# Router logits from the unnormalised residual, the shared expert split around the ranking and among the routed experts, and a smaller table of relative biases

## The chip, the cores and the metric

The kernel runs on one core of one Trainium2 chip. The metric is the device time of one launch in microseconds (us). Five engines work side by side: TensorE (PE, with its weight loads PEld), VectorE (DVE), ScalarE (ACT), GpSimd (POOL) and SyncE (SP, which here only issues transfers). They wait for one another through semaphores.

## The reference, cut to what matters

Two blocks run one after the other on 512 tokens of width 1024, in float32. The first has a gated mixer, attention with a relative bias, and two convolutional feed-forwards. The second has two more mixers and then a mixture of experts:

```
h = rms_norm(x, norm2_g) * (1 + sc2) + sh2
scores = sigmoid(h @ router_w)                      # 64 experts
sel = scores + router_bias                          # choice: 4 of 8 groups, then 6 experts
idx = top_6(sel in the 4 best groups)
wts = scores[idx] / sum(scores[idx]) * 2.5
routed = sum over idx of wts * swiglu(h, exp_w[idx])
shared = swiglu(h, sh_w_gate, sh_w_up, sh_w_down)   # for every token, inner width 256
x = x + g2 * (routed + shared);  out = rms_norm(x, final_g)
```

The attention of the first block adds `b_rel_bias[head, distance]` to its scores, for 16 heads and distances up to 256.

## The kernel before, in words

Activations lie transposed in on-chip memory: features on the 128 partitions, in 8 blocks (`KB`), and the 512 tokens along the free dimension. One float32 product of a 128x128 weight tile with 512 columns is shown as two matmul records. A transpose of 128x128 is one record.

Order is set by hand. Each engine has one program, and `s("name")` with a count says what it waits for. Four places matter here.

The table of relative biases. GpSimd writes the 16 x 384 row `relR` 128 times per head to `rel_dram` (3 MB), then reads it back skewed as `biasT` (128 partitions, 2 MB), lines 625 to 630. In that time the "gv" stage runs: TensorE takes four units of `a_w_in` of 1 MB through a ring of two buffers (L940). SyncE issues the load of a unit when the buffer's last reader is done (L438).

The first output projection, "go" (L845). The weights come in four units of two output blocks each. The first four output blocks are computed together, k by k over `gT`, as VectorE produces it; the load of the third unit waits for the first unit's two outputs.

The norm of the second block (L1083 to L1095), then the projections (L1104) that follow a short chain on ACT and DVE.

The router stage. VectorE adds the last projection to x (L2424). ACT squares it (L1604), GpSimd sums six blocks (L641), TensorE sums over partitions (L827). ACT takes the root, VectorE the reciprocal of 128x512 (L2165) and the eight scalings (L2167), ACT the shifts (L1615). TensorE then computes the logits (L1417), turns the tokens for the gather (L1428), runs the shared gate and up products (L1436), the counts (L1443, L1445), the shared down products in pieces (L1458), the places of the tokens (L1491, L1498, L1501), and turns the result back (L1514). VectorE ranks (L2446 to L2468) meanwhile. Then come 44 expert units (L1531 gate and up, L1544 down). Units 0 to 3 have one expert with 128 slots, and after them units with two experts of 64 slots and units with one expert alternate. SyncE keeps four buffers of 3 MB filled: the two parts for the expert four places later are loaded when `exp_gu` and `exp_down` say that they are free (L505).

Of the kernel before, what the change touches and what calls it, by code (L numbers as in the profile page):

```python
# [91 lines left out]
def program(nc, a, out):  # L92

    with ExitStack() as ctx:
# [35 lines left out]
        rel_dram = scratch("rel_dram", 16, P, RELW + 1)  # L130
# [86 lines left out]
        sh_gu, sh_dn = flat_ring[:, 1024:5120], sqf[:, 2048:4096]  # L217
        hrow = [flat_ring[:, 1024 + D * n:1024 + D * n + D] for n in range(2)]
# [35 lines left out]
        xact = sqf[:, 0:1024].rearrange("p (b t) -> p b t", b=2)  # L254
# [156 lines left out]
        OV = 15  # L411

# [11 lines left out]
        def _(sp):  # L424
# [87 lines left out]
            for q in range(2):  # L512
                expert_in(q, bass.ds(q, 1), sems_of(q), slice(0, 3))
            expert_in(2, bass.ds(2, 1), sems_of(2), GU)
# [4 lines left out]
            expert_in(2, bass.ds(2, 1), sems_of(2), DN)  # L519
            sp.wait_ge(s("norm_ss_ready"), nth("n2"))  # L520
            sp.dma_start(sh_dn.rearrange("p (k n) -> p k n", k=2),
                         a["sh_w_down_2"][0].rearrange("(k p) n -> p k n", p=P)).then_inc(s("sh_loaded"), 16)
            sp.wait_ge(s("front_stored"), 48)
            expert_in(3, bass.ds(3, 1), sems_of(3), GU)
            sp.wait_ge(s("sh_prod"), 4 + KB)
            expert_in(3, bass.ds(3, 1), sems_of(3), DN)

            sp.wait_ge(s("rt_step"), 7)
# [37 lines left out]
        def _(pool):  # L566
# [37 lines left out]
            for n in range(6):  # L604
# [26 lines left out]
            pool.wait_ge(s("rel_stored"), 32)  # L631
# [3 lines left out]
            def square_sums(n):  # L635

                for b in range(1, KB - 1):
# [100 lines left out]
            square_sums("n2")  # L738
# [39 lines left out]
            pool.wait_ge(s("sh_prod"), 4)  # L778
# [12 lines left out]
            gather(0)  # L791
            gather(1)
            pool.wait_ge(s("sh_prod"), 4 + KB)
# [25 lines left out]
        def _(pe):  # L819
# [272 lines left out]
            pe.wait_ge(s("side_loaded"), 64)  # L1092
            for k in range(KB):
# [317 lines left out]
            mean_squares("n2")  # L1411
            pe.wait_ge(s("side_loaded"), 64)
            for t in range(TT):
                for k in range(KB):
                    if t == 0:
                        pe.wait_ge(s("norm_h_ready"), h_count("n2", k))
                    mm = pe.matmul(ps[0][:, t * 64:t * 64 + 64], hT[:, k, t * P:(t + 1) * P], rwt[:, k, :],  # L1417
                                   start=(k == 0), stop=(k == KB - 1))
            mm.then_inc(s("rt_prod"), 1)

            pe.wait_ge(s("mod_ready"), ADA_UNITS)
            pe.transpose(ps[1][0:8, 0:P], mod[:, 40:48], ident[:]).then_inc(s("rt_prod"), 1)

            for t in range(TT):
                for half in range(2):
                    wait(pe, s("tokens_taken"), 2 * (t - 1) + half + 1)
                    for b in range(4):
                        tr = pe.transpose(ps[2 + half][:, b * P:(b + 1) * P], hT[:, 4 * half + b, t * P:(t + 1) * P], ident[:])  # L1428
                    tr.then_inc(s("tokens_turned"), 1)

            pe.wait_ge(s("sh_loaded"), 48)
            w8 = sh_gu.rearrange("p (m k n) -> p m k n", m=2, k=KB)
            for m in range(2):
# [1215 lines left out]
```

## Time and profile before

| | us |
|---|---|
| three runs | 2834.86, 2831.92, 2834.57 (median 2834.57) |
| profiled execution, its own time | 2836.34 |
| its span | 2834.6 |
| TensorE busy | 2641.1 (93%) |
| VectorE busy | 839.5 (30%) |
| mean granted TensorE clock | 0.971 |

The span is the traced part of the profiled execution, 1.7 us shorter than its own time. Lines as L906 are lines of the kernel file. "Idle before" is the time for which the engine stood still ahead of a group, with what released it. A granted clock of 1.00 is 2.4 GHz, one of 0.50 is 1.2 GHz.

### The profile page before, as it was taken

The page shows a single profiled execution, that of the slowest core. Times are in us where ns is not written, and L with a number is a line of the kernel's source. Part 1 is how long each engine was busy: PE and PEld are TensorE (multiplying, and loading weights), DVE is VectorE, ACT ScalarE, POOL GpSimd, SP SyncE. Part 2 cuts the span into 40 slices and gives each one's busy share as a digit, 9 for nine tenths or more (in the row PEclk, how much of TensorE's full clock was granted, in tenths as well). Part 3 has the DMA queues.
Part 4 walks back from the last instruction along what each step waited for, and adds up shares of the span by engine and source line. Part 5 has one row for each costly group of instructions (what it writes and reads, how often), then busy time and mean ns, then how long its engine had stood idle before and what let it go on. Part 6 is the DMA issues. An engine that isn't in the chain of part 4 may idle for free. (4 is left out here: it accounts for less than half of the span.)

```text
span 2834.6 us, 27215 instructions
## 1 busy us (share of the span) xinstructions
PE 2641.1 (93%) x9849; PEld 1370.8 (48%) x9849; DVE 839.5 (30%) x1957; ACT 578.4 (20%) x1076; POOL 441.6 (16%) x397
## 2 busy tenths in 40 slices
PE   6999999999999999999999989999989999999992
PEld 5544444444566444444444447666745444344440
DVE  1023222102333232220022335556533322222215
ACT  2111111111333211110025533122111211111111
POOL 3004555500000100000121001101110111111110
PEclk9999999999999999999999999999988999999996
DMA  7315555432121122233232110000032799999985
GB/s 144 118 60 146 147 148 148 138 82 62 49 60 60 60 74 74 81 85 82 63 82 75 40 49 25 25 30 16 23 154 91 263 419 417 404 400 400 389 349 215
DMA packets 290831, 407.24 MB, mean 144 GB/s; under 512 B 14258, under 2 KB 253560, under 8 KB 264608
## 3 DMA queue, kind: packets, MB, share of 16 engines
q1 hardware_dynamic: 273504, 366.24, 37.3%
q0 software_dynamic: 16112, 37.19, 4.5%
q10 hardware_dynamic: 1104, 2.31, 0.2%
q8 instruction: 71, 1.16, 0.2%
q14 instruction: 40, 0.33, 0.0%
HBM read 396.20 MB, written 30.46 MB: 151 GB/s over the span
## 5 line engine op out<-in xcount | busy, mean ns | idle before, releaser
L906 PE MATMUL bank<-hT,bring 128*128 128x512 f32 x1344 | 582.1, 593 | 0.0
L906 PEld LDWEIGHTS bank<-hT,bring 128*128 128x128 f32 x1344 | 253.8, 190 | 311.9 <-issue 311.9
L845 PE MATMUL bank<-bring 128*128 128x512 f32 x704 | 303.3, 593 | 0.0
L1531 PE MATMUL bank<-bring 128*64 128x512 f32 (+1 forms) x512 | 227.0, 596 | 2.7 <-issue 1.7
L845 PEld LDWEIGHTS bank<-bring 128*128 128x128 f32 x704 | 133.5, 190 | 166.5 <-issue 166.5
L2023 DVE SCALAR_TENSOR_TENSOR ffw<-bank,col,ffw 128x511 f32<-128x511 f32 x88 | 66.0, 750 | 413.5 <-ACT ffw L1632 413.3
L1632 ACT ACTIVATE ffw<-bank,col 128x512 f32<-128x512 f32 x88 | 68.5, 778 | 492.7 <-PE bank L906 470.0
L2008 DVE TENSOR_TENSOR xT<-bank,xT 128x512 f32<-128x512 f32 x32 | 22.1, 691 | 377.3 <-PE bank L845 377.2
L1544 PE MATMUL bank<-bring,xT 128*64 128x512 f32 (+1 forms) x256 | 120.3, 614 | 9.1 <-DMA ysq<-exp_w_down 4.5
L1531 PEld LDWEIGHTS bank<-bring 128*64 128x64 f32 (+1 forms) x512 | 77.8, 157 | 97.4 <-issue 96.2
L1104 PE MATMUL bank<-hT,bring 128*128 128x512 f32 x256 | 118.5, 610 | 3.6 <-DVE ysq L2188 3.6
L641 POOL TENSOR_TENSOR ysq<-ysq 128x512 f32<-128x512 f32 x24 | 30.5, 1269 | 583.4 <-ACT ysq L1604 582.3
L1531 PE MATMUL bank<-ysq,bring 128*64 128x512 f32 (+1 forms) x256 | 113.4, 596 | 2.8 <-issue 2.8
L2563 DVE TENSOR_TENSOR xT<-bank,ysq 128x512 f32<-128x512 f32 x88 | 60.9, 692 | 180.1 <-PE bank L1544 180.1
L1531 PE MATMUL bank<-two,bring 128*64 128x512 f32 (+1 forms) x256 | 113.4, 596 | 0.5 <-issue 0.4
L1953 ACT ACTIVATE xT<-bank 128x256 f32<-128x256 f32 x44 | 16.9, 385 | 468.2 <-PE bank L1531 468.2
L735 POOL TENSOR_TENSOR ffw<-two,maskT 128x512 f32<-128x512 f32 x40 | 52.2, 1314 | 385.6 <-DVE two L2362 318.6
L656 POOL TENSOR_TENSOR two<-two,csil 128x2048 f32<-128x2048 f32 x24 | 86.5, 3604 | 154.9 <-DMA two<-ada_w 137.7
L658 POOL TENSOR_TENSOR two<-two 128x1024 f32<-128x1024 f32 (+2 forms) x72 | 104.2, 1447 | 5.6
L784 POOL DMA_INDIRECT bring<-h_dram,slot_token x44 | 44.9, 1020 | 366.9 <-DVE slot_token L2526 347.3
L1199 PE MATMUL bank<-hT,bring 128*128 128x512 f32 x192 | 92.4, 617 | 2.4 <-ACT bring L1824 2.4
L2559 DVE TENSOR_TENSOR xT<-bank,xT 128x256 f32<-128x256 f32 x44 | 18.7, 425 | 252.9 <-ACT xT L1953 252.9
(475 smaller groups left out, 3604.2 us busy)
## 6 DMA issues: line engine op xcount, KB each, us to landing
bring<-f_w_in SPq DMA_DIRECT2D x88, 512.0 KB, 5.2
bring<-exp_w_gate SPq DMA_DIRECT2D x32, 1024.0 KB
bring<-exp_w_up SPq DMA_DIRECT2D x32, 1024.0 KB
bring<-exp_w_down SPq DMA_DIRECT2D x32, 1024.0 KB
two<-ada_w SPq DMA_DIRECT2D x24, 1024.0 KB, 5.4
bring<-f_w_down SPq DMA_DIRECT2D x16, 1408.0 KB, 6.9
two<-exp_w_gate SPq DMA_DIRECT2D x16, 1024.0 KB
two<-exp_w_up SPq DMA_DIRECT2D x16, 1024.0 KB
```

What stands on the lines that cost most here:

```text
L656: step(1, nc.gpsimd.tensor_tensor(w, w, csil[:].unsqueeze(2).to_broadcast([P, KB, 256]), ALU.mult))
L658: step(k, nc.gpsimd.tensor_tensor(w[:, 0:n, :], w[:, 0:n, :], w[:, n:2 * n, :], ALU.add))
L735: nc.gpsimd.tensor_tensor(Am[h], ABT[h][:, :, 0:P], bc4(maskT[n][:]), ALU.mult)\
L845: mm = pe.matmul(ps[BANKS[stage][n % 4]][:], w[:, k, n % per * P:(n % per + 1) * P], rhs[:, k, :], start=(k == 0), stop=(k == kb - 1))
L906: mm = pe.matmul(ps[2 * j + b][:], w[:, k, b * P:(b + 1) * P], hT[:, k, :], start=(k == 0), stop=(k == KB - 1))
L1104: mm = pe.matmul(ps[n % 2][:], slot(n // 2, 8, 256)[:, k, n % 2 * P:(n % 2 + 1) * P], hT[:, k, :], start=(k == 0), stop=(k == KB - 1))
L1199: mm = pe.matmul(ps[(0, 7, 6)[m]][:], w, hT[:, k, :], start=(k == 0), stop=(k == KB - 1))
L1531: mm = pe.matmul(ps[3][m * h:m * h + m, :].rearrange("p (m n) -> p m n", m=2), hgT[par][:, k, m * h:m * h + m], w, start=(k == 0), stop=(k ...
L1544: mm = pe.matmul(ps[5 + half][m * h:m * h + m, :], eactT[par][:, k * P + m * h:k * P + m * h + m], exw[b][:, 4096 + k * D + half * 512:409 ...
L1632: nc.scalar.activation(conv[j][b], ps[2 * j + b][:], ACT.Identity, scale=col[:, bass.ds(c0 + P + blk, 1)], bias=col[:, bass.ds(c0 + P + 44 ...
L2023: nc.vector.scalar_tensor_tensor(out=c[:, 1:T], in0=ps[2 * j + b][:, 0:T - 1], scalar=col[:, bass.ds(c0 + 44 + blk, 1)], in1=c[:, 1:T], op ...
L2563: return nc.vector.tensor_tensor(yrow[par][:, cols], ps[5 + half][:], g2_row[:, cols], ALU.mult)
```

## The change

There are four edits.

1. The table in `rel_dram` has 16 rows per head instead of 128, and `biasT` is read in eight transfers of 16 partitions each.
2. In "go" two output blocks are computed together instead of four.
3. The router's logits come from `gmod * x`, before the norm is known: ACT writes this into `hT` block by block right behind its squares, and the logits are scaled by the token's 1/rms afterwards, with `lbias = rwt^T sh2` added. `lbias` is computed once, in the norm stage of the second block (8 products of 64 columns). The 1/rms comes from 12 products of one column and is spread over the partitions by 4 products of 128 columns. VectorE multiplies `hT` by it in parts, ACT shifts in parts. GpSimd sums five blocks instead of six.
4. The shared gate and up products are issued k by k, four k ahead of the counts and four behind the places. The shared down products leave this stage: for units 12 to 19 one step of two products (tokens on partitions, 512 features) follows each unit, and VectorE adds it to `res` with two operations. The result is turned back ahead of that. SyncE loads the shared weights ahead of experts 1 and 2, and the down weights into `rstd`, `spare`, `rel` and `prow`.

The core of the diff:

```diff
-        rel_dram = scratch("rel_dram", 16, P, RELW + 1)
+        rel_dram = scratch("rel_dram", 16, 16, RELW + 1)
...
-            pool.dma_start(rel_dram[:, :, 0:RELW], relR[:].unsqueeze(1).to_broadcast([16, P, RELW]))\
+            pool.dma_start(rel_dram[:, :, 0:RELW], relR[:].unsqueeze(1).to_broadcast([16, 16, RELW]))\
...
-            pool.dma_start(biasT, bass.AP(rel_dram.tensor, 127, [[RELW, P], [P * (RELW + 1), 16], [1, 256]]))\
-                .then_inc(s("rel_stored"), 16)
+            for p in range(0, P, 16):
+                pool.dma_start(biasT[p:p + 16], bass.AP(rel_dram.tensor, P - 1 - p, [[RELW, 16], [16 * (RELW + 1), 16], [1, 256]]))\
+                    .then_inc(s("rel_stored"), 16)
...
             for k in range(KB):
-                for n in range(4):
+                for n in range(2):
                     pe.wait_ge(s("vn_ready"), TT + max(k, n) + 1)
                     linear_step("go", gT, KB, n, k)
-            linear("go", gT, KB, lambda k: None, done=[KB] * 4)
+            linear("go", gT, KB, lambda k: None, done=[KB] * 2)
...
+            for k in range(KB):
+                mm = pe.matmul(ps[5][:, 0:EXPERTS], mod[:, 24 + k:25 + k].to_broadcast([P, P]), rwt[:, k, :],
+                               start=(k == 0), stop=(k == KB - 1))
...
+            for k in range(KB):
+                pe.wait_ge(s("raw_ready"), 4 * KB + k + 1)
+                for t in range(TT):
+                    mm = pe.matmul(ps[2 + t][:, 0:EXPERTS], hT[:, k, t * P:(t + 1) * P], rwt[:, k, :],
+                                   start=(k == 0), stop=(k == KB - 1))
+                if k == 3:
+                    ...
+                    for t in range(TT):
+                        for b in (0, KB - 2, KB - 1):
+                            total = pe.matmul(ps[7][:, t:t + 1], sq[:, b, t * P:(t + 1) * P], mean[:, 0:1],
+                                              start=(b == 0), stop=(b == KB - 1))
+                    total.then_inc(s("norm_ss_ready"), 1)
...
+            for t in range(TT):
+                mm = pe.matmul(ps[0][:, t * P:(t + 1) * P], row_inv[:, t:t + 1].to_broadcast([P, P]), ident[:], start=True, stop=True)
...
+            def shared_down(d):
+                t, half = divmod(d, 2)
+                wait(pe, s("sh_added"), d)
+                for k in range(2):
+                    mm = pe.matmul(ps[7][:], xact[:, k, t * P:(t + 1) * P], sh_dn[k][half], start=(k == 0), stop=(k == 1))
+                mm.then_inc(s("sh_prod"), 1)
...
+                if u in SHARED_UNITS:
+                    shared_down(u - SHARED_UNITS[0])
...
+            act_e.wait_ge(s("side_prod"), 6)
+            nc.scalar.copy(row_factor, ps[0][:]).then_inc(s("front_act"), 1)
+            act_e.wait_ge(s("rt_step"), 1)
+            nc.scalar.activation(sco, sco, ACT.Sigmoid).then_inc(s("front_act"), 1)
+            shift("n2", 24, range(4))
...
+            def scaled(blocks):
+                for b in blocks:
+                    nc.vector.tensor_tensor(hT[:, b, :], hT[:, b, :], row_factor, ALU.mult).then_inc(s("h_scaled"), 1)
...
+                order(nc.vector.tensor_tensor(sh_part, ps[7][:], g2_row[:, cols], ALU.mult))
+                nc.vector.tensor_tensor(res[:, t, cols], res[:, t, cols], sh_part, ALU.add).then_inc(s("sh_added"), 1)
```

On TensorE, from the last products of the output projection (L1223) on, there stands before:

```order
L1223 MATMUL bank<-ysq,bring 128x512 x9
L827 MATMUL bank<-ysq,mean 128x512 x2
L1417 MATMUL bank<-rwt,hT 128x64 x32
L1422 MATMUL bank<-ident,mod 8x128
L1428 MATMUL bank<-ident,hT 128x128 x32
L1436 MATMUL bank<-hT,bring 128x512 x32
L1443 MATMUL bank<-two,maskT 128x64 x4
L1445 MATMUL bank<-onec,two 64x1 x4
L1449 MATMUL bank<-ident,ffw 64x128 x4
L1458 MATMUL bank<-ysq 128x512 x8
L1488 MATMUL bank<-ffw 1x64
L1491 MATMUL bank<-ffw,rms 128x64 x4
```

and now, where L1232 is that projection, L1425 the logits, L1433 and L1439 the norm, L1451 the shared gate and up, L1461 the turned tokens:

```order
L1232 MATMUL bank<-ysq,bring 128x512 x9
L1425 MATMUL bank<-rwt,hT 128x64 x16
L1433 MATMUL bank<-mean,ysq 128x1 x12
L1425 MATMUL bank<-rwt,hT 128x64 x16
L1439 MATMUL bank<-ident,ss 128x128 x4
L1442 MATMUL bank<-ident,mod 8x128
L1451 MATMUL bank<-hT,bring 128x512 x16
L1470 MATMUL bank<-two,maskT 128x64 x4
L1472 MATMUL bank<-onec,two 64x1 x4
L1461 MATMUL bank<-ident,hT 128x128 x16
L1478 MATMUL bank<-ident,ffw 64x128 x4
L1505 MATMUL bank<-ffw 1x64
```

The logits have moved ahead of the norm and half of the shared gate and up products behind the places; the shared down products (L1458 before) are gone from here.

On TensorE at the end of unit 12 and in unit 13, where L1544 (before) and L1567 (now) are the down products:

```order
L1544 MATMUL bank<-two,xT 64x512
L1531 MATMUL bank<-bring 128x512 x8
L1477 MATMUL bank<-ident,bring 128x128 x4
L1469 MATMUL bank<-ffw 128x2
L1471 MATMUL bank<-ffw 128x2 x4
L1537 MATMUL bank<-ident,xT 128x128 x2
L1477 MATMUL bank<-ident,bring 128x128 x4
L1544 MATMUL bank<-bring,xT 128x512 x4
L1531 MATMUL bank<-ysq,bring 64x512
L1531 MATMUL bank<-bring 64x512
```

The same place now:

```order
L1567 MATMUL bank<-two,xT 64x512
L1545 MATMUL bank<-rstd,bring 128x512
L1545 MATMUL bank<-rel,bring 128x512
L1554 MATMUL bank<-bring 128x512 x8
L1496 MATMUL bank<-ident,AR 128x128 x4
L1488 MATMUL bank<-ffw 128x2
L1490 MATMUL bank<-ffw 128x2 x4
L1560 MATMUL bank<-ident,xT 128x128 x2
L1496 MATMUL bank<-ident,AR 128x128 x4
L1567 MATMUL bank<-bring,xT 128x512 x4
L1545 MATMUL bank<-spare,bring 128x512
L1545 MATMUL bank<-prow,bring 128x512
```

Two products of 512 columns (L1545, the shared down) now follow each of the units 12 to 19.

On GpSimd at the table of biases before:

```order
L622 DMA rwt<-router_w 128x8x64
L623 DMA rbias<-router_bias 128x64
L626 DMA rel_dram<-rel 2048x1x384
L629 DMA two<-rel_dram 128x16x256
L633 MEMSET two 64x16x64
```

And now:

```order
L626 DMA rwt<-router_w 128x8x64
L627 DMA rbias<-router_bias 128x64
L630 DMA rel_dram<-rel 256x1x384
L634 DMA two<-rel_dram 16x16x256 x8
L638 MEMSET two 64x16x64
```

The write has 256 rows instead of 2048, and eight reads stand in the place of one.

## Rows read from the trace of the kernel before

**Rows 1.** The page, busy time of each engine and share of the span

```profile
PE 2641.1 (93%) x9849; PEld 1370.8 (48%) x9849; DVE 839.5 (30%) x1957; ACT 578.4 (20%) x1076; POOL 441.6 (16%) x397
```

**Rows 2.** Timeline, first value stage: start, duration, engine, line, operation, [idle before]

```profile
32.38 27.79 PE L940 MATMUL bank<-bring,ysq 128*128 128x256 f32 x128
...
39.30 1.05 POOL L626 DMA_DIRECT2D rel_dram<-rel  x1 [12.78 <-DVE rel L2060]
...
76.74 15.95 PE L940 MATMUL bank<-bring,ysq 128*128 128x256 f32 x64 [16.57 <-DMA bring<-a_w_in]
...
92.53 13.90 PE L969 MATMUL bank<-hT,bring 128*128 128x512 f32 x32
```

**Rows 3.** DMA issues up to 200 us: count, size, median us to landing

```profile
bring<-a_w_in SPq DMA_DIRECT2D x8, 1024.0 KB, 7.7
...
bring<-a_w_out SPq DMA_DIRECT2D x4, 1024.0 KB, 5.0
...
rel_dram<-rel POOLq DMA_DIRECT2D x1, 3072.0 KB, 35.1
...
two<-rel_dram POOLq DMA_DIRECT2D x1, 2048.0 KB, 10.8
```

**Rows 4.** Timeline, the first output projection

```profile
156.15 27.63 PE L845 MATMUL bank<-two,bring 128*128 128x512 f32 x64
...
187.40 30.59 PE L845 MATMUL bank<-two,bring 128*128 128x512 f32 x64 [3.62 <-DMA bring<-a_w_out]
```

**Rows 5.** Timeline, TensorE ahead of the second block projections

```profile
1437.04 5.11 PE L1083 MATMUL bank<-small,ysq 128*128 128x2 f32 x32 [2.15 <-ACT ysq L1748]
...
1442.96 3.44 PE L1089 MATMUL bank<-ident,ss 128*128 128x128 f32 x16 [0.81 <-DVE ss L2172]
...
1446.72 7.03 PE L1095 MATMUL bank<-hT,favw 128*24 128x512 f32 x16 [0.33 <-ACT hT L1615]
...
1457.33 16.78 PE L1104 MATMUL bank<-hT,bring 128*128 128x512 f32 x32 [3.58 <-DVE ysq L2188]
```

**Rows 6.** Timeline, the router stage, TensorE and VectorE

```profile
2111.44 3.68 PE L827 MATMUL bank<-ysq,mean 128*128 128x512 f32 x4 [3.91 <-POOL ysq L641]
...
2120.92 15.48 PE L1417 MATMUL bank<-rwt,hT 128*128 128x64 f32 x64 [5.80 <-ACT hT L1615]
...
2136.41 4.59 PE L1428 MATMUL bank<-ident,hT 128*128 128x128 f32 x24
...
2136.93 0.43 DVE L2446 TENSOR_TENSOR two<-two,rbias 128x256 f32<-128x256 f32 x1 [12.27 <-ACT two L1908]
...
2147.88 0.42 DVE L2468 TENSOR_TENSOR ffw<-ffw,two 128x256 f32<-128x256 f32 x1
...
2169.86 1.00 PE L1443 MATMUL bank<-two,maskT 128*128 128x64 f32 x8
...
2204.09 2.41 PE L1531 MATMUL bank<-bring 128*128 128x512 f32 x5 [0.99 <-ACT hT L1940]
```

**Rows 7.** Stretches of the router stage: busy us by engine, then TensorE clock

```profile
2121.00:2136.00 15.00, 15.00 (x64) 13.94 (x65) 3.66 (x6) 5.70 (x8) 0.00 (x0) 0.50 0.65 237
...
2142.00:2170.00 28.00, 28.00 (x71) 12.69 (x71) 6.55 (x18) 3.56 (x5) 0.00 (x0) 1.00 0.37 139
...
2187.00:2190.00 3.00, 3.00 (x27) 2.78 (x25) 0.00 (x0) 0.00 (x0) 0.00 (x0) 1.00 0.00 0
```

**Rows 8.** Eight expert units each, columns as above, then DMA share, GB/s

```profile
2261.44:2361.89 100.45, 97.67 (x412) 41.36 (x410) 25.39 (x92) 15.45 (x32) 16.14 (x16) 1.00 1.01 414
...
2361.89:2470.13 108.24, 99.31 (x411) 43.58 (x409) 25.37 (x92) 15.44 (x32) 16.13 (x16) 0.98 1.00 410
...
2470.13:2577.66 107.53, 97.95 (x412) 43.92 (x410) 25.39 (x93) 15.44 (x32) 16.14 (x16) 1.00 0.98 399
```

**Rows 9.** The page, one VectorE operation on 128x512 with its mean duration

```profile
L2008 DVE TENSOR_TENSOR xT<-bank,xT 128x512 f32<-128x512 f32 x32 | 22.1, 691 | 377.3 <-PE bank L845 377.2
```

More of the change, by code:

```diff
@@ L1419, in _ @@
[L1419 to L1429, printed above, removed]
@@ L1441, in _ @@
+            for k in range(4):
+                shared_gate_up(k)
+            pe.wait_ge(s("rt_step"), 2)
             pe.wait_ge(s("moe_consts"), 26)
@@ L1450, in _ @@
             tr.then_inc(s("rt_prod"), 1)
-            wd = sh_dn.rearrange("p (k n) -> p k n", k=2)
-            pe.wait_ge(s("rt_step"), 4)
-            def shared_down(b):
-                wait(pe, s("sh_added"), b - 3)
-                for k in range(2):
-                    mm = pe.matmul(ps[4 + b % 4][:], wd[:, k, b * P:(b + 1) * P], xact[:, k, :],
-                                   start=(k == 0), stop=(k == 1))
-                mm.then_inc(s("sh_prod"), 1)
             def slots(u):
@@ L1609, in squares, with shift @@
                 nc.scalar.activation(rms[:], ps[7][:], ACT.Sqrt, bias=epsc[:]).then_inc(s("norm_rms_ready"), 1)
-            def shift(n, c):
-                for b in range(KB):
+            def shift(n, c, blocks=range(KB)):
+                for b in blocks:
                     act_e.wait_ge(s("h_scaled"), KB * (n == "n2") + b + 1)
@@ L1903, in _ @@
             result_roots(3)
-            squares("n2", "lin_added", 5 * KB)
-            shift("n2", 24)
-            act_e.wait_ge(s("rt_prod"), 1)
-            nc.scalar.activation(sco, ps[0][:, 0:256].rearrange("p (t e) -> p t e", t=TT), ACT.Sigmoid)\
-                .then_inc(s("front_act"), 1)
+            for b in range(KB):
+                act_e.wait_ge(s("lin_added"), 4 * KB + b + 1)
+                nc.scalar.activation(sq[:, b, :], xT[:, b, :], ACT.Square).then_inc(s("norm_sq_ready"), 1)
+                nc.scalar.activation(hT[:, b, :], xT[:, b, :], ACT.Identity, scale=gmod[:, 8 + b:9 + b]).then_inc(s("raw_ready"), 1)
@@ L1911, in _, with take_tokens @@
+            shift("n2", 24, range(4))
             act_e.wait_ge(s("rt_prod"), 2)
-            order(nc.scalar.copy(g2T, ps[1][0:8, 0:P]))
+            nc.scalar.copy(g2T, ps[3][0:8, 0:P]).then_inc(s("tokens_taken"), 1)
+            act_e.wait_ge(s("tokens_taken"), 1)
             act_e.dma_start(g2_dram, g2T).then_inc(s("front_stored"), 16)
-            for t in range(TT):
-                for half in range(2):
-                    act_e.wait_ge(s("tokens_turned"), 2 * t + half + 1)
+            def take_tokens(half):
+                for t in range(TT):
+                    act_e.wait_ge(s("tokens_turned"), 4 * half + t + 1)
@@ new lines, in take_tokens @@
+                    if half and t % 2:
+                        act_e.wait_ge(s("tokens_taken"), t + 6)
+                        act_e.dma_start(h_dram[(t - 1) * P:(t + 1) * P, :].rearrange("(t p) d -> p t d", p=P),
+                                        htok[:, t - 1:t + 1, :]).then_inc(s("front_stored"), 16)
+            take_tokens(0)
+            shift("n2", 24, range(4, 6))
+            act_e.wait_ge(s("rt_prod"), 4)
+            nc.scalar.copy(nthT, ps[0][0:EXPERTS, :]).then_inc(s("front_act"), 1)
@@ L1923, in _ @@
+            shift("n2", 24, range(6, KB))
+            take_tokens(1)
             for b in range(2):
@@ L1945, in _ @@
                 rows_turned(0, half)
-            for m in range(4, 2 * TT):
-                take_result(m)
             for u in range(len(UNITS)):
```

222 lines of the change are left out of this document (119 added, 103 removed).

## The prediction

> **What bounds the kernel now.** I read the page first: TensorE is busy for 2641.1 of 2834.6 us [rows 1], so nearly every gain must be idle time of TensorE, a low clock, or work that leaves its program. I then went along its timeline to the places of the change and looked for idle time that a transfer or another engine ends.
>
> Up to 100 us there is one large stall. The products of the value stage take 27.79 us for two units, so 13.9 each; they end at 60.2, and TensorE stands still for 16.57 us until a load of `a_w_in` lands [rows 2]. A load of that size lands in 7.7 us as a rule. This one was issued at 46.3, when its buffer came free in the middle of the 27.79 us, and took 30 us. What was moving then is the 3 MB write of the table, issued at 39.3, which landed 35.1 us later, at 74.4 [rows 2, 3]. The load landed 2.3 us after that. The write starved it. After the stall the last unit takes 15.79 us (92.53 less 76.74) instead of 13.9, at the low clock.
>
> The first output projection has a smaller stall of the same kind: 3.62 us until `a_w_out` lands, since the first buffer is freed only when all four output blocks end. The second half then takes 30.4 us where the first took 27.63 for the same 64 records [rows 4].
>
> In the router stage TensorE ends the projection at 2107.5 (2111.44 less 3.91) and starts the first expert unit at 2204.1, 96.6 us later [rows 6]. The logits take 15.48 us of it, all at a granted clock of 0.50, though TensorE was busy for the whole stretch [rows 6, 7]. The ranking on VectorE starts at 2136.93 and ends at 2148.3, 11.4 us; TensorE reaches the counts, which need it, at 2169.86 [rows 6]. So the ranking is hidden by the shared gate and up products, and TensorE's own work bounds the stage.
>
> In the expert units two limits lie close together. Units 4 to 11 take 100.45 us, 12.56 each, with the DMA engines full. Units 12 to 19 take 108.24 and units 20 to 27 take 107.53 with the same products, so about 7 to 8 us in each eight are waits for weights [rows 8].
>
> **The table.** The small write is an eighth of the old one: 35.1 / 8 = 4.4 us; with its issue it lands near 46, and GpSimd issues the first of eight reads at about 46.5. The starving write is gone, but the 2 MB of reads now move at the moment at which it mattered: they start together with the load of `a_w_in`. Their price is not in the trace. One bound is the old read, 2 MB to 128 partitions in 10.8 us [rows 3]: they end at 57.5, the load lands by 60, and the stall goes: 92.53 less (60.2 + 13.9) = 18.4 us gained, clock loss included. The other is the rate of the old write, whose on-chip side has 16 partitions, as each of the new reads has: 3 MB in 35.1 us, so 2 MB in 23.4 us. They end at 70, the load lands 2.3 us later, at 72.2, and 4.5 us are gained. I take 21.5 us for the reads, the load at 70.5 and a gain of 6.2, near the second bound, because the nearest row in shape is the write with 16 partitions.
>
> The Trainium skill has a rule on this that speaks against the change ("SBUF — State Buffer", section on the DMA port swizzle): bandwidth depends on how many of 16 ports the partitions reach, and by its table any 16 neighbouring partitions reach four. The trace agrees as far as it goes: 90 GB/s for the write against 194 GB/s for the read to 128 partitions. By the page's 435 GB/s for all ports the reads would take 19 us, an estimate, and the gain would be about 8 us.
>
> **"go".** The first buffer is free after half of the first 27.63 us, and its 5.0 us load has the other 13.8 us to hide in. VectorE's pace in `gT` does not bind: 64 records ran without a gap behind it [rows 4], though two blocks per k need it faster. Gain: 3.62 us of stall and 30.4 less 27.63 = 2.8 us of clock, 6.4 us. Bounds: 3.6 if the low clock stays, 6.4.
>
> **`lbias`.** Eight products of 64 columns go between L1089 and L1095, where TensorE idles for only 0.33 us [rows 5]. At 0.22 us each at full clock (27 records in 3.00 us) or 0.48 at the low one (64 records in 15.48) [rows 6, 7] that is 1.8 to 3.9 us. Behind L1095 TensorE waits for VectorE (L2188), which has work of its own in this time and hides part. I take 1.0 us of loss; bounds 0 and 3.6.
>
> **The router stage.** From 2107.5 on, in TensorE's new order. Logits: 32 products. The raw blocks are written by ACT right behind the squares, so the first half starts at once, at 0.22 us each, 3.6 us. I expect the clock to fall during it, as it had fallen to 0.50 in L1083, which has short products too, and stayed there through L1417 [rows 5, 7]; the other half then costs 0.48 each, 7.7 us. Norm: 12 products of one column at L1083's 5.11 / 16 = 0.32 us, 3.8 us. Spread: half of L1089's 3.44 us, 1.7 us. Then a new exposed chain before the first shared product: ACT copies, VectorE scales, ACT shifts, at about 0.7 us each [rows 9] and some latency, 2.2 us. Shared gate and up: the same 32 products, which ran from 2142.3 to 2169.9, 27.6 us, and 1.7 us more since the first four start at the low clock. Tokens turned: 6.0 us as before (2136.4 to 2142.4). From the counts to the first unit there were 34.2 us (2204.09 less 2169.86); eight shared down steps leave, 16 products at 28.0 / 32 = 0.87 us [rows 7], 13.9 us, and 20.3 us stay, among them the two waits and clock falls that the stage has now. One wait is new there: `nthT` is copied by ACT behind four token copies and two shifts, and TensorE has nothing in between: 2.0 us.
>
> Sum: 3.6 + 7.7 + 3.8 + 1.7 + 2.2 + 27.6 + 1.7 + 6.0 + 20.3 + 2.0 = 76.6 us instead of 96.6: a gain of 20.0 us. The ranking (11.4 us) starts about 2 us ahead of the first of four k of shared products (3.5 us each, 15.5 with the low clock) and stays hidden. If that cover is too short, 2 to 3 us come on top. Bounds: all logits, norm and spread at full clock and no wait for `nthT`, 30 us gained; all logits at the low clock (15.5) and 3 us of ranking exposed, 13 us gained.
>
> The rule of the Trainium skill ("TensorE: Matmul & The Clock Gate", "What's actually happening") is that the slow clock is the default and activity releases it. By it, logits that follow straight on the projection would keep the full clock and the gain would be at the upper bound. The trace disagrees in part: 15 us of unbroken short products stayed at 0.50 [rows 7]; so I do not count on it.
>
> The earlier stage also loads less ahead of the shared weights (3 MB instead of 8 MB), so they come early. The weights of experts 1 and 2 come later but have more than 40 us. I cost this at nothing.
>
> **The shared down steps among the units.** 8 x 2 x 0.87 = 13.9 us of TensorE. Units 12 to 19 would take 8 x 12.56 + 13.9 = 114.4 us at least, 6.2 more than the 108.24 with their waits. While TensorE is slower than the loads, the loads get ahead again, as they were before units 4 to 11, and these ran for eight units without waits. So units 20 to 27 can fall from 107.53 to 100.5, 7.0 less. Net: -0.8, I take 1 us gained. Bounds: 5 us gained (waits further on vanish too), 14 us lost (nothing is hidden). VectorE's two operations of 0.69 us a unit [rows 9] lie beside it (25.4 us busy in 100).
>
> **Sum.** -6.2 - 6.4 + 1.0 - 20.0 - 0.8 = -32.4 us. The profiled execution took 2836.3, so 2803.9; the median of the runs is 1.8 us lower, so 2802.
>
> **Rivals.** A: the table's reads are fast. For: the old read took 10.8 us. Against: the 90 GB/s of the 16-partition write. The gain is 18.4 instead of 6.2: 2790.
>
> B: the shared down steps are not hidden, because the loads can only get four buffers ahead and the freed time is lost on the DMA side. For: DMA share 1.00 in rows 8, so lost time does not come back. Against: units 4 to 11, which lived on such a lead. 14 us lost instead of 0.8 gained: 2817.
>
> C: the router stage gains only its lower bound, since the ranking and ACT's queue (copies, shifts, `nthT`) become the bound where TensorE was: 13 instead of 20, 2809.
>
> D, slower than before: each of the eight reads to 16 partitions costs what the whole old read did, 10.8 us. They then end at 46.5 + 86.4 = 133, the load lands at 135, and TensorE waits 75 us instead of 16.57, 58.5 us more than now, with the loads of the next units starved alike. With the other terms (-26.2) the time is 2836.3 - 26.2 + 58.5 - 1.8 = 2867. It decides from 6.8 us a read on. For: DMA share was full in the old write at a quarter of the usual rate. Against: the write moved 256 KB in 2.9 us.
>
> **Chances.** Forecast 0.45, A 0.35, B 0.08, C 0.09, D 0.03. The range takes in A with a router stage a few us better, and half of B: 2783 to 2814. A measurement of this kernel can tell 0.2% (5.7 us) from no change. All cases but D are faster by more: faster 0.96, within 0.2% 0.01, slower 0.03.
>
> **What would show it.** In the changed profile: the eight reads landing near 68 and TensorE's wait in the value stage near 10 us (A: gone; D: tens of us); no wait for `a_w_out`; the logits' second half at clock 0.50; the first expert unit starting 20 us sooner after the projection's end than now; units 12 to 19 near 114 us with no DMA wait, units 20 to 27 near 100. The prediction is wrong in its reasoning if the value stage's wait ends for another reason than the load, if the counts wait for the ranking, or if units 20 to 27 still take 107 us.

## The result and the profile after

The changed kernel takes 2789.5 us in the median (2788.6 to 2790.9, four runs), the kernel before 2833.2 us in the same comparison (2827.9 to 2834.9). The ratio is 0.9847, with a 95% interval of 0.9831 to 0.9862. The forecast was 2802 us, with a range of 2783 to 2814. The gain is 43.7 us between the medians and 47.7 us between the two profiled executions (2836.34 and 2788.59), where 32.4 were forecast.

The table follows TensorE's program through both traces.

| stretch | before, us | after, us | gain | forecast |
|---|---|---|---|---|
| value stage, to the start of the next products | 92.53 | 85.86 | 6.7 | 6.2 |
| first output projection, start to end | 61.8 | 55.1 | 6.7 | 6.4 |
| norm of the second block (L1083 or L1087, to the start of the projections) | 20.3 | 20.3 | 0 | -1.0 |
| from there to the projection's end, where TensorE's program is unchanged | 650.2 | 643.5 | 6.7 | 0 |
| projection's end to the first expert unit | 96.6 | 69.9 | 26.6 | 20.0 |
| first unit to the start of the last | 564.0 | 563.2 | 0.8 | 0.8 |

TensorE in the value stage of the changed kernel, in the timeline (start, duration, engine, line, operation, idle before):

```profile
32.44 27.79 PE L944 MATMUL bank<-bring,ysq 128*128 128x256 f32 x128
69.84 16.19 PE L944 MATMUL bank<-bring,ysq 128*128 128x256 f32 x64 [9.61 <-DMA bring<-a_w_in]
85.86 13.90 PE L973 MATMUL bank<-hT,bring 128*128 128x512 f32 x32
```

and GpSimd there:

```profile
39.37 0.59 POOL L630 DMA_DIRECT2D rel_dram<-rel  x1 [12.91 <-DVE rel L2096]
45.70 4.47 POOL L634 DMA_DIRECT2D two<-rel_dram  x8 [5.74 <-DMA rel_dram<-rel]
70.20 0.94 POOL L638 MEMSET two<- 64x1024 f32 x1 [20.03 <-DMA two<-rel_dram]
```

The rows answer to [rows 2]. The write now lands in 6.0 us and the wait is 9.61 us instead of 16.57. The wait still ends with the load of `a_w_in`, at 69.8, just before the last read of the table has landed (the memset that waits for all eight starts at 70.20). The eight reads took 24.5 us from the first issue. These are the numbers of one execution. In the seven profiled kernels that have these reads at this place they took 21.0 to 24.5 us, the wait was 6.2 to 9.6 us, and the next products started at 82.9 to 86.3.

The first output projection [rows 4] is one unbroken piece, 128 records without a wait:

```profile
149.48 55.10 PE L849 MATMUL bank<-two,bring 128*128 128x512 f32 x128
```

TensorE in the router stage, again in the timeline; the rows answer to [rows 6]:

```profile
2087.24 3.68 PE L1425 MATMUL bank<-rwt,hT 128*128 128x64 f32 x32
2090.76 2.79 PE L1433 MATMUL bank<-mean,ysq 128*128 128x1 f32 x24
2093.41 5.79 PE L1425 MATMUL bank<-rwt,hT 128*128 128x64 f32 x32
2098.99 2.02 PE L1439 MATMUL bank<-ident,ss 128*128 128x128 f32 x8
...
2103.32 16.53 PE L1451 MATMUL bank<-hT,bring 128*128 128x512 f32 x32 [2.09 <-ACT hT L1640]
2119.69 1.00 PE L1470 MATMUL bank<-two,maskT 128*128 128x64 f32 x8
...
2126.03 1.10 PE L1508 MATMUL bank<-ffw,rms 64*128 64x64 f32 x8 [1.74 <-ACT rms L1961]
2127.76 3.46 PE L1513 MATMUL bank<-two,maskT 128*128 128x64 f32 x20 [0.64 <-DVE order_tab L2526]
2131.02 3.71 PE L1461 MATMUL bank<-ident,hT 128*128 128x128 f32 x16
...
2139.80 10.52 PE L1451 MATMUL bank<-hT,bring 128*128 128x512 f32 x24
...
2157.34 7.11 PE L1554 MATMUL bank<-bring 128*128 128x512 f32 x16 [0.77 <-ACT bring L1974]
```

The logits follow the projection without a gap, the first half in 3.5 us. The ranking ended at 2115.5 on VectorE, 4 us before TensorE reached the counts (L1470). The granted clock of four stretches (length, busy us of PE, PEld, DVE, ACT and POOL, then the clock):

```profile
2087.30:2090.80 3.50, 3.50 (x34) 3.50 (x32) 0.79 (x2) 3.27 (x6) 3.14 (x6) 1.00 0.79 287
2093.40:2099.00 5.60, 5.60 (x35) 5.60 (x34) 0.18 (x1) 1.75 (x3) 0.00 (x0) 0.63 1.06 403
2103.30:2119.70 16.40, 16.38 (x33) 7.12 (x34) 12.59 (x66) 1.85 (x4) 0.00 (x0) 0.84 0.59 239
2124.30:2139.80 15.50, 13.14 (x70) 10.29 (x71) 4.05 (x19) 6.54 (x10) 0.00 (x0) 0.78 0.34 133
```

The first half of the logits runs at full clock, and so does the norm behind it (1.00 from 2090.80 to 2093.40). In the second half it falls, and the first shared products start low.

The expert units, cut at the same places as [rows 8]:

```profile
2214.66:2315.11 100.45, 97.67 (x412) 41.36 (x410) 25.35 (x92) 15.42 (x32) 16.10 (x16) 1.00 1.01 414
2315.11:2430.08 114.97, 111.40 (x444) 47.63 (x442) 36.97 (x108) 15.41 (x32) 16.07 (x16) 1.00 0.97 398
2430.08:2531.01 100.93, 97.75 (x412) 41.99 (x410) 25.36 (x93) 15.42 (x32) 16.09 (x16) 1.00 1.00 408
```

Units 12 to 19 take 6.7 us more than before and hold 12.1 us more of TensorE's busy time; units 20 to 27 take 6.6 us less.

### The profile page after: what moved, and what is told of

It reads as the page before. It is cut to its first block and busy times, and to the rows that moved or that the text cites. A ratio compares the mean times of both kernels' runs of the same rounds, so it can differ in the third digit from the quotient of the medians.

```text
span 2786.5 us, 27348 instructions
## 1 busy us (share of the span) xinstructions
PE 2626.5 (94%) x9893; PEld 1364.1 (49%) x9893; DVE 842.5 (30%) x1970; ACT 581.8 (21%) x1086; POOL 442.4 (16%) x403
## 5 line engine op out<-in xcount | busy, mean ns | idle before, releaser
L1567 PE MATMUL bank<-bring,xT 128*64 128x512 f32 (+1 forms) x256 | 117.2, 600 | 5.7 <-DMA two<-exp_w_down 3.1
L792 POOL DMA_INDIRECT y_dram<-xT,slot_row x44 | 43.9, 998 | 203.1 <-DVE xT L2603 194.4
```

The source lines that it names most:

```text
L1567: mm = pe.matmul(ps[5 + half][m * h:m * h + m, :], eactT[par][:, k * P + m * h:k * P + m * h + m], exw[b][:, 4096 + k * D + half * 512:409 ...
```

## Experiments

Twelve kernels ran. All ratios are to the kernel before, timed on the same chip in the same comparison; its medians there were 2831.7, 2829.7 and 2832.9 us.

**The table alone.**

```diff
--- the kernel before
-        rel_dram = scratch("rel_dram", 16, P, RELW + 1)
+        rel_dram = scratch("rel_dram", 16, 16, RELW + 1)
... (one read of biasT becomes eight of 16 partitions)
```

> The kernel before with the first edit alone: 16 rows per head in the table and eight reads of 16 partitions. If the stages add up, the value stage does what it does in the changed kernel: the eight reads land near 70 us, TensorE waits 9.6 us for the load of a_w_in instead of 16.6, and the time falls by 6.7 us (92.53 less 85.86), to a ratio near 0.9976. Rival: the gain seen in the changed kernel's value stage is given back later (another load comes late, or the clock falls elsewhere): a ratio of 0.999 to 1.001.

Measured: 2825.0 us, ratio 0.9974 (0.9963 to 0.9985). The wait is 6.46 us in this execution, and the next products start at 83.57. What follows: the gain stands by itself and is not given back, since the interval leaves out the rival's 0.999.

**"go" alone.**

```diff
--- the kernel before
-                for n in range(4):
+                for n in range(2):
...
-            linear("go", gT, KB, lambda k: None, done=[KB] * 4)
+            linear("go", gT, KB, lambda k: None, done=[KB] * 2)
```

> The kernel before with the second edit alone: two output blocks of the first output projection together instead of four. My step says 3.6 us of wait and 2.8 us of low clock go, 6.4 us; the changed kernel's stage took 54.9 us instead of 61.8, so 6.9 us: a ratio of 0.9975. Rival: the low clock is not due to the wait and stays, 3.6 us and a ratio of 0.9987, with a stage of 58 us.

Measured: 2824.9 us, ratio 0.9976 (0.9966 to 0.9987). The stage is one piece of 55.10 us. So the low clock went with the wait. The interval reaches the rival's 0.9987, but the rival's stage of 58 us is excluded by the trace.

**The changed kernel without these two edits.**

```diff
--- the changed kernel: table and "go" as in the kernel before
-        rel_dram = scratch("rel_dram", 16, 16, RELW + 1)
+        rel_dram = scratch("rel_dram", 16, P, RELW + 1)
...
-                for n in range(2):
+                for n in range(4):
```

> The changed kernel with edits 1 and 2 undone (the old table with one read, four output blocks together). If the edits add up it is 13.6 us slower than the changed kernel, near 2803 us, a ratio to the kernel before of 0.989 to 0.990. The changed kernel's trace has 6.8 us less between the norm of the second block and the router stage, where no edit acts: if that is the clock's chance, it may come or go here and the ratio may be 0.992; if it follows from an edit of the router stage (the products of lbias), it is here too.

Measured: 2804.6 us, ratio 0.9903 (0.9885 to 0.9921), 27 us faster than before. The router stage takes 69.9 us, as in the changed kernel. 6.7 + 6.8 + 27.1 are 40.6 us from the three separate medians, against 43.7 for all together; the intervals cover the rest. The forecast (0.989 to 0.990) and its alternative (0.992) both lie inside the interval.

The 6.7 us gained between the norm stage and the projection's end are here too: the stretch takes 643.4 us, while the norm stage ahead of it takes 23.6 us instead of 20.3. The traces of all kernels tell more. The stretch took 650.2, 647.4 and 647.0 us in the three profiled kernels without edit 3, 643.4 to 644.6 in ten of the eleven with it, and 647.5 in the eleventh. In the three and in the eleventh the granted clock is at 0.50 for 6.8 of the last 60 us of the projection, and in the ten it is 1.00 throughout. So part of the gain goes with edit 3, although nothing of TensorE's program is changed in this stretch; by what way is open, and the eleventh kernel shows that the pattern of the clock can also change without it. The rest is the draw of one execution: in 23 executions the kernel before ranged from 2827.1 to 2840.5 us with mean clocks of 0.976 to 0.971, and the profiled one (2836.34 us, 0.971) was among the slower. The medians don't decide how large the part of the edit is, since the interval of this kernel is 10 us wide.

**Reads that reach every eighth partition.**

```diff
--- the changed kernel
-            for p in range(0, P, 16):
-                pool.dma_start(biasT[p:p + 16], bass.AP(rel_dram.tensor, P - 1 - p, [[RELW, 16], ...
+            for p in range(8):
+                pool.dma_start(biasT[p:P:8], bass.AP(rel_dram.tensor, P - 1 - p, [[RELW - 7, 16], ...
```

> The changed kernel with the eight reads of the table writing to every eighth partition (p, p+8, ..., p+120) instead of to 16 neighbours; same bytes, same number and size of packets, same queue. If the neighbouring partitions are what makes the reads take 24 us in all, they now take about the 10.8 us of the old read to 128 partitions, end near 57 us, the load of a_w_in lands by 60 us, TensorE's wait of 9.6 us goes and its unit takes 13.9 us instead of 16.2: 12 us less, near 2777.6 us, a ratio to the kernel before of 0.980. Rival: the reads are slow because they go through one queue in eight pieces, or because their rows overlap in memory: no change, a wait of 9.6 us, a ratio of 0.9847.

Measured: 2779.4 us, ratio 0.9815 (0.9798 to 0.9832), 10 us below the changed kernel between the medians. TensorE and GpSimd there:

```profile
63.88 14.08 PE L944 MATMUL bank<-bring,ysq 128*128 128x256 f32 x64 [2.67 <-DMA bring<-a_w_in]
77.80 13.90 PE L973 MATMUL bank<-hT,bring 128*128 128x512 f32 x32
```

```profile
46.26 4.46 POOL L634 DMA_DIRECT2D two<-rel_dram  x8 [5.33 <-DMA rel_dram<-rel]
63.36 0.94 POOL L638 MEMSET two<- 64x1024 f32 x1 [12.64 <-DMA two<-rel_dram]
```

Same queue, packets and bytes; the partitions differ, and with them the place in each row of the table at which a read starts. The reads end 17.1 us after their first issue instead of 24.5, and the wait falls from 9.61 to 2.67 us. So the layout matters, and eight pieces in one queue can't be the whole reason, as the rival has it. But they did not become as fast as the old read (10.8 us), so the last 2.7 us of wait stayed.

**The same, but after the load.**

```diff
--- the kernel with reads of every eighth partition
+            pool.wait_ge(s("gv_prod"), 13)
             for p in range(8):
```

> The changed kernel with the reads to every eighth partition, and issued only when the first product group of the fourth unit of the value stage is done, so when all four loads of a_w_in have landed. The reads then meet only the load of the next stage, which has 14 us to spare. TensorE's wait of 2.7 us in the value stage, which was left with the reads spread, goes: 2777 us, 2.5 us below the spread reads and 12 below the changed kernel, a ratio of 0.9805. Rival: the wait comes back in the next stage, because the load that meets the reads is late there: 2779.5 us or more, a ratio of 0.9815.

Measured: 2780.3 us, ratio 0.9822 (0.9806 to 0.9838). The value stage has no wait left and the next products start at 74.74, 3.1 us earlier than with the spread reads; but the medians do not differ. The gain in the place is shown, a gain in the whole is not.

**Late reads of neighbouring partitions.**

```diff
--- the changed kernel
+            pool.wait_ge(s("gv_prod"), 13)
             for p in range(0, P, 16):
```

> The changed kernel with its eight reads of 16 neighbouring partitions as they are, but issued only when the first product group of the fourth unit of the value stage is done. If the layout alone sets how long the reads take, they take 20 to 25 us also here, where no waiting load stands beside them (with the reads spread over the partitions they took 13.5 us at this place); they end near 88 us. The load that is issued at 74 us is then starved until about 90 us, and the stage that follows has a wait of 0 to 3 us; the time is 2780 to 2783 us, a ratio of 0.982 to 0.983. Rival: the reads were slow because they and the load of a_w_in held each other up; alone they take about 13 us, as the spread ones.

Measured: 2781.4 us, ratio 0.9817 (0.9803 to 0.9830). GpSimd in this kernel, then in the one with late reads of every eighth partition:

```profile
64.03 4.47 POOL L635 DMA_DIRECT2D two<-rel_dram  x8 [24.36 <-PE bank L945]
83.45 0.94 POOL L639 MEMSET two<- 64x1024 f32 x1 [14.94 <-DMA two<-rel_dram]
```

```profile
65.11 4.46 POOL L635 DMA_DIRECT2D two<-rel_dram  x8 [24.31 <-PE bank L945]
78.57 0.94 POOL L639 MEMSET two<- 64x1024 f32 x1 [9.00 <-DMA two<-rel_dram]
```

2 MB take 19.4 us with neighbours and 13.5 us when spread, with no stalled load beside them. So the layout costs 6 us by itself. The meeting with the load costs 2 to 5 us more (21.0 to 24.5 less 19.4), and 3.6 us when the reads are spread (17.1 less 13.5). The load that is issued at 73.8 us, beside these reads, lands at 86.2. The next stage had no wait. Moving the reads out of the way is worth as much as spreading them.

**All shared gate and up products ahead of the counts.**

```diff
--- the changed kernel
-            for k in range(4):
+            for k in range(KB):
                 shared_gate_up(k)
...
-            shared_gate_up(4)
...
-            for k in range(5, KB):
-                shared_gate_up(k)
... (VectorE's scalings and ACT's shifts move ahead with them, so that no shift stands ahead of the copy of nthT)
```

> The changed kernel with all eight k of the shared gate and up products ahead of the counts (VectorE scales and ACT shifts all eight blocks before the ranking), nothing else. In the changed kernel the stage from the projection's end to the first unit took 70.0 us where I had 76.6, and most of the difference lies behind the counts. If that is because four k of products now stand there and cover the waits and keep the clock up, the stage becomes 4 to 5 us longer, near 2794 us, a ratio to the kernel before of 0.986 to 0.987. Rival: the order is indifferent, since the same products are issued, and the waits behind the counts are fixed by other engines: 2789.5 us within 1.5, a ratio of 0.9847.

Measured: 2796.5 us, ratio 0.9877 (0.9858 to 0.9895), and the stage takes 77.6 us, 7.7 more. The direction was right and the reason was wrong. One of TensorE's waits (us in total, times, the longest), and then GpSimd and TensorE in the timeline:

```profile
PE bank L1496 <- DMA AR<-h_dram,slot_token: 7.5, 1, 7.5
```

```profile
2150.34 1.13 POOL L788 DMA_INDIRECT AR<-h_dram,slot_token  x1 [60.33 <-DMA h_dram<-ysq]
```

```profile
2159.30 1.94 PE L1496 MATMUL bank<-ident,AR 128*128 128x128 f32 x8 [7.50 <-DMA AR<-h_dram,slot_token]
```

What was added is one wait, for the first gather of tokens. ACT issues the last write of tokens to `h_dram` at 2143.8, the write is complete 6.5 us later, the gather starts, and its rows are used 9.0 us after that. In the kernel before, the tokens were turned ahead of everything, and this chain was long done. The changed kernel turns them late, and what hides the chain is the second half of the shared products.

**Six k ahead, two behind.** The edit is the one above with `range(6)` and `range(6, KB)`, and six scalings and shifts ahead.

> The changed kernel with six k of the shared gate and up products ahead of the counts and two behind the places, instead of four and four. Putting all eight ahead cost 7.5 us of wait for the first gather of tokens, which starts when the last tokens are written and took 9 us from its issue. In the changed kernel the same chain would end 3.4 us before its rows are needed. Two k less behind the places take 7.2 us of cover away: if that chain is the cause, TensorE waits 3 to 4 us for the gather, and the time is 2793 us, a ratio of 0.986. Rival: the wait comes with the whole order and not with the cover: 0 or 7.5 us of wait.

Measured: 2788.8 us, ratio 0.9850 (0.9834 to 0.9866); the stage takes 70.1 us and has no wait for the gather. GpSimd and TensorE in this kernel:

```profile
2145.48 1.13 POOL L788 DMA_INDIRECT AR<-h_dram,slot_token  x1 [53.45 <-DMA h_dram<-ysq]
```

```profile
2154.24 0.60 PE L1496 MATMUL bank<-ident,AR 128*128 128x128 f32 x4
```

My 3 to 4 us of wait were wrong. I had taken the gather at 9.0 us, and here it landed in 7.5, at 2153.0, 1.2 us before its rows were needed. In the changed kernel it is issued at 2142.67 and lands at 2150.1, 5.0 us before 2155.08. So the chain is the cause of the 7.5 us of the last experiment, and the cover shrinks as it should (5.0, 1.2, then a wait), but two k are cover enough. The stage's length alone would not show it, since two other waits changed as well: the one for `nthT` is 0.51 us instead of 1.74, because no shifts stand ahead of its copy, and TensorE waits 1.23 us for VectorE (L2531), where the changed kernel computes shared products.

**The shared down steps elsewhere.**

```diff
--- the changed kernel
-        SHARED_UNITS = range(12, 20)
+        SHARED_UNITS = range(4, 12)      # and, in another kernel, range(34, 42)
```

> The changed kernel with the eight shared down steps behind units 4 to 11 instead of 12 to 19. Theory: the steps are free only where loads can use the time to get ahead. At unit 4 all four buffers are full, so 13.9 us of TensorE are added there and the loads wait for buffers; units 12 to 19 then lose their waits (8 us) and units 20 to 27 keep theirs: 6 to 7 us slower than the changed kernel, near 2796 us, a ratio of 0.987. Rival: the whole stretch is bound by the DMA engines and any place in it hides the steps: 2789.5 us, a ratio of 0.9847.

> The changed kernel with the eight shared down steps behind units 34 to 41. Loads need about 13.35 us a unit there and TensorE 12.56, so each step of 1.73 us finds 0.8 us of wait; the rest would let the loads get ahead, but only two units are left to use that. Of 13.9 us about 8 are hidden, and the time is 6 us above the changed kernel, near 2795.5 us, a ratio of 0.9868. Rival: as with units 12 to 19, all is hidden: 2789.5 us; or none is: 2803 us, a ratio of 0.9895.

**And left out.** Here the product with `sh_w_down` and its addition are not computed.

```diff
--- the changed kernel
-        SHARED_UNITS = range(12, 20)
+        SHARED_UNITS = (99,)
```

> The changed kernel without the eight shared down steps: the product of the shared expert with sh_w_down and its addition are left out, 13.9 us of TensorE. If they are fully hidden by waits for weights, the waits come back (units 12 to 19 near 108 us, units 20 to 27 near 107.5) and the time is 2789.5 to 2791 us, a ratio of 0.9847. Rival: some of the 13.9 us is paid in the changed kernel: 2 to 6 us less.

The times of the units, from the starts in the timelines:

| us | 0 to 11 | 12 to 19 | 20 to 27 | 28 to the start of 43 | sum | ratio |
|---|---|---|---|---|---|---|
| before | 150.3 | 108.3 | 107.5 | 198.0 | 564.0 | 1 |
| steps at 12 to 19 (changed) | 150.2 | 115.0 | 100.9 | 197.0 | 563.2 | 0.9847 |
| steps at 4 to 11 | 164.0 | 100.5 | 106.4 | 197.9 | 568.7 | 0.9878 |
| steps at 34 to 41 | 150.2 | 108.1 | 108.0 | 207.1 | 573.5 | 0.9891 |
| steps left out | 150.2 | 108.0 | 108.3 | 198.6 | 565.0 | 0.9861 |

The medians were 2795.1 us (interval of the ratio 0.9857 to 0.9898), 2799.6 (0.9872 to 0.9910) and, left out, 2792.6 (0.9845 to 0.9876). With the steps left out TensorE's waits for weights are back, here those for down weights (us in total, times, the longest):

```profile
PE bank L1567 <- DMA bring<-exp_w_down: 7.7, 7, 1.5
...
PE bank L1567 <- DMA ysq<-exp_w_down: 4.7, 4, 1.6
PE bank L1567 <- DMA two<-exp_w_down: 4.4, 4, 1.3
```

against these in the changed kernel:

```profile
PE bank L1567 <- DMA bring<-exp_w_down: 4.2, 4, 1.2
PE bank L1567 <- DMA two<-exp_w_down: 3.1, 3, 1.1
PE bank L1567 <- DMA ysq<-exp_w_down: 2.2, 2, 1.3
```

13.9 us of TensorE's work at units 12 to 19 cost nothing: without it the units take 1.9 us more and the median is 3.1 us higher, with intervals that overlap, so this can't be told from zero. At 4 to 11 the work is paid in full where it stands (13.7 us), and 8.9 us come back as waits that vanish behind it (100.5 and 106.4 us where it was 108.3 and 107.5); the DMA share in units 4 to 11 falls to 0.96, as it would if loads waited for a buffer:

```profile
2207.33:2321.51 114.18, 111.40 (x442) 47.42 (x441) 36.17 (x107) 15.42 (x32) 16.22 (x17) 1.00 0.96 385
2321.51:2421.96 100.45, 97.68 (x410) 41.35 (x409) 26.13 (x93) 15.41 (x32) 15.96 (x16) 1.00 1.00 407
```

The second to last number of a row is the DMA share. At 34 to 41 the units take 10.3 us more than in the changed kernel, where I expected 6: of the 13.9 us only about 5 found a wait (207.1 us where the kernel without the steps has 198.6), and no units follow that could use a lead.

**Late reads, and `nthT` copied first.**

```diff
--- the kernel with late reads of every eighth partition
-            shift("n2", 24, range(4, 6))
             act_e.wait_ge(s("rt_prod"), 4)
             nc.scalar.copy(nthT, ps[0][0:EXPERTS, :]).then_inc(s("front_act"), 1)
+            shift("n2", 24, range(4, 6))
```

> The changed kernel with the late reads to every eighth partition, and with ACT copying nthT ahead of the shifts of blocks 4 and 5 instead of behind them. The copy starts 1.1 us sooner, so the wait of 1.74 us for it becomes about 0.6 us; with the value stage without a wait the time is 2778 us, a ratio of 0.981, the lowest of all. Rival: the shifts of the later blocks become late for the tokens' second half, and nothing is gained over the late reads alone, 2780 us.

Measured: 2778.2 us, ratio 0.9808 (0.9794 to 0.9821), the lowest of all kernels here and 11 us below the changed one. The stage takes 65.2 us instead of 69.9, four times the 1.1 us that I expected. The same pieces as at 2126 above:

```profile
2118.42 1.10 PE L1509 MATMUL bank<-ffw,rms 64*128 64x64 f32 x8 [0.51 <-ACT rms L1961]
2120.16 2.44 PE L1514 MATMUL bank<-two,maskT 128*128 128x64 f32 x20 [0.64 <-DVE order_tab L2527]
2122.44 1.04 PE L1462 MATMUL bank<-ident,hT 128*128 128x128 f32 x8
```

and the clock over the same work as 2124.30 to 2139.80 in the changed kernel:

```profile
2117.92:2129.39 11.47, 10.10 (x70) 7.64 (x71) 4.05 (x19) 6.33 (x10) 0.00 (x0) 1.00 0.38 149
```

The wait is 1.2 us shorter, and the clock stays at 1.00 where it was 0.78 on average: 15.50 us become 11.47. A further 0.9 us comes from the first half of the shared products (15.67 us instead of 16.53), ahead of the edit.

How much of the 4.7 us the edit brought is not shown. This is the kernel that stood out above: in its execution the clock had gone another way already ahead of the edit. The stretch up to the projection's end took 3.5 us more than in the kernel with late reads (647.5 and 644.0), and the clock was 0.89 instead of 0.84 over the first half of the shared products. The two kernels with eight and with six k ahead have the short wait for `nthT` too (0.52 and 0.51 us), and there the clock was 0.77 over the 15 us from L1508 on, as in the eight kernels with the long wait. Only the twenty records right behind the wait (L1513) follow its length everywhere: 3.3 us at 1.74 us of wait, in eight kernels, and 2.3 us at 0.51 or 0.52, in three. The medians of the kernels with and without the edit show 2.1 us, with intervals that hold both, and the 1.1 us that I expected are not excluded.

## Why the prediction was right, and where it was not

The table (forecast 6.2, measured 6.7). The step was right in mechanism and size: the reads do meet the load, they took 24.5 us where I took 21.5 (21.0 to 24.5 in seven kernels), and the load landed with them instead of 2.3 us behind. That the 6.7 lies so close is in part luck, since the same reads left waits of 6.2 to 9.6 us. That it was the other transfers that held the load up is shown by the three kernels with late reads: there it lands in 5.3 to 5.5 us, against 30.3 us beside the old write and 23.3 us beside the reads. The "7.7 us as a rule" of the prediction is a median that includes loads which something held up; no term hangs on it. Choosing the slow bound, by the partitions of the nearest row, was right, and rival A (fast reads, 2790 us) is out, although its time came true: the total met it for other reasons. That 16 neighbouring partitions are slow is now shown by the pair of late reads, 19.4 and 13.5 us. The Trainium skill's rule on this ("SBUF — State Buffer", the section on the DMA port swizzle) gave 19 us as an estimate; the reads with nothing stalled beside them took 19.4. By its table, in which 16 neighbours that start at a multiple of 16, like the ones here, reach four ports, a read of every eighth partition reaches eight ports instead of four, so half of that time, 9.6 us as an estimate; the trace has 13.5, of which the eight issues alone are 4.5 us. The direction agrees, the ratio is less than the rule gives.

"go" (forecast 6.4, measured 6.7 in the trace, 6.8 between medians). Right, low clock included.

`lbias` (forecast a loss of 1.0, measured 0). Without the products the time from L1083 to the same place 60 us on was 61.7 us in three traces; with them 60.0 to 64.7 in eleven, 61.6 on average. The idle time behind it fell from 3.58 to 2.24 us and the first projections after it took 14.00 us instead of 16.78.

The router stage (forecast 20.0, measured 26.6) holds the term that failed. The logits' first half, the spread and the exposed chain came out within 0.1 us. The second half of the logits took 5.6 instead of 7.7 us, since the clock fell only 1.4 us into it (0.63 on average), and the norm 2.65 instead of 3.8: the stage kept the full clock longer behind the projection than the 0.50 of [rows 7] had made me expect. The shared products took 30.8 us instead of 29.3. The mis-sized term is the "20.3 us that stay" from the counts to the first unit, with 2.0 for `nthT`: measured 17.4 instead of 22.3. I had carried the old waits and clock falls over as a block. In the old order they came from the shared down steps and their additions; in the new one four k of products stand there. The wait for `nthT` was there as forecast (1.74 us, with 2.0 taken), and the records right behind it took 1 us longer than behind a short wait.

What I had not seen is the chain of the tokens: written, gathered and used within 20 us, hidden only because half of the shared products moved behind it. It cost nothing in this kernel, but "tokens turned, 6.0 us as before" was the whole of my step, and a split at eight would have lost 7.5 us by it.

The shared down steps (forecast a gain of 0.8, measured 0.8; 115.0 and 100.9 us in place of the 114.4 and 100.5 forecast). Right, by the mechanism given: rival B is excluded by the kernel without the steps. At units 4 to 11, where the lead is full, rival B holds in part: 5.6 of the 13.9 us are lost. Rivals C and D are out: the ranking never bound the stage, and the eight reads took 24.5 us together, 3.1 each.

The total was forecast 12.5 us too high: 6.6 from the router stage, 2.3 from the terms ahead of it and the tail, and the other 3.6 from the stretch at which I had counted nothing. It gained 6.7 us between the two profiles, of which about 3 are taken up by the 1.8 us that I had already taken off and by the distance of the changed kernel's profile from its median. The sum started from the profile of before, which drew more low clock than most executions: I had allowed 1.8 us between it and the median of three runs, and the median of 23 is 4.6 us below it. What else the stretch gained goes with edit 3 by a way that is open, and the prediction has no term for it.

## What to carry to other kernels

Work that leaves a bound stage is free only in a stretch where the engine waits for loads and the loads have room to get ahead; eight units too early 5.6 of the 13.9 us were lost, and near the end, where nobody is left to use the lead, 10 us. When products are reordered, write down the whole chain through memory (write, its completion, gather, use), since what covers it may be the very work that moves. A short wait between short products can cost more than its length, because the products behind it can run at the low clock: order the copy that TensorE waits for ahead of those that it does not. And look at the clock ahead of an edit before you credit the edit with a stage that got shorter: one profiled execution can differ by several us there.

## What the runs showed of the hardware

Eight reads of 256 KB to 16 neighbouring partitions took 19.4 us, to every eighth partition 13.5 us, with the same packets, queue and bytes. A 1 MB load that lands in 5.3 to 5.5 us with nothing beside it took 30.3 us beside a 3 MB write from 16 partitions and 23.3 us beside eight narrow reads. Behind a wait of 1.74 us the next twenty short records took 3.3 us, in eight kernels, and 2.3 us behind a wait of 0.51 or 0.52 in three. Logits that follow straight on a projection kept the granted clock of 1.00 through 16 products and a norm of 12, and it fell in the next 16. And the clock's falls differ from execution to execution of one kernel: 23 executions spread over 13 us, in step with mean clocks between 0.971 and 0.976.
